# Projection rows streamed through TensorE from the last token to the first, odd weight buffers 128 bytes later

## What is computed

```python
h = rmsnorm(x, norm_mix_g[l])
proj = jnp.einsum('btd,dn->btn', h, w_in[l])
(a_u, a_v, b_q, b_k, b_v, b_z, b_beta, b_alpha, c_q, c_k, c_v, gates) = jnp.split(proj, splits, axis=-1)
...
gates = jax.nn.sigmoid(gates.reshape(B, T, N_BRANCH, D))
```

## Time and profile before

| | us |
|---|---|
| median of 3 runs | 1966.67 |
| lowest, highest | 1965.94, 1969.8 |
| the profiled execution | 1968.53 |
| its span, first to last instruction | 1966.8 |
| TensorE busy in it | 1911.2 |
| VectorE busy | 1093.6 |
| ScalarE busy | 957.7 |
| GpSimd busy | 322.9 |

### The profile page before, as it was taken

The page is one execution under the profiler, slowest core; times in us unless marked ns, Lnnn a source line. Parts: engine busy times, 40 slices in busy tenths (PEclk is TensorE's granted clock), DMA queues, the critical chain, the costliest instruction groups (busy, mean ns, idle before and its releaser), DMA issues.

```text
span 1966.8 us, 26385 instructions
## 1 busy us (share of the span) xinstructions
PE 1911.2 (97%) x9734; PEld 1609.0 (82%) x9734; DVE 1093.6 (56%) x1343; ACT 957.7 (49%) x1301; POOL 322.9 (16%) x483
## 2 busy tenths in 40 slices
PE   6999999999999999999999999999999999999994
PEld 6998888888888888888898788877888888888872
DVE  5113755343442323131246575349988988889865
ACT  5233334222334555554256022135877787877862
POOL 1000000002132232311001000002222222332220
PEclk9999999999999999999999999989999999999997
DMA  6323335799445453534576964246999999999956
GB/s 230 114 91 107 113 122 207 282 350 338 129 155 170 156 183 131 179 115 143 185 225 217 355 228 150 86 192 242 389 381 387 394 390 389 393 387 383 380 202 261
DMA packets 169762, 468.61 MB, mean 238 GB/s; under 512 B 27775, under 2 KB 57423, under 8 KB 163788
## 3 DMA queue, kind: packets, MB, share of 16 engines
q1 hardware_dynamic: 131020, 373.60, 51.3%
q0 software_dynamic: 28288, 74.95, 11.3%
q10 hardware_dynamic: 10368, 18.88, 2.8%
HBM read 378.51 MB, written 105.61 MB: 246 GB/s over the span
## 4 chain that ended last, share of the span: by engine, by line
PE 92%; DVE 3%; DMA 2%; ACT 1%; issue 1%; SPq 0%; POOL 0%; DVEq 0%; POOLq 0%; ACTq 0%
PE psum L668 26%; PE psum L670 26%; PE psum L669 26%; PE psum L2385 2%; PE psum L2361 2%; PE psum L2729 1%; PE psum L2371 1%; PE psum L2398 1%; PE psum L2653 1%; DVE e_l L2135 1%; PE psum L2331 1%; PE psum L2751 1%; PE psum L2789 1%; PE psum L2790 1%; DMA y_raw<-y_scratch 1%
## 5 line engine op out<-in xcount | busy, mean ns | idle before, releaser
L2135 DVE TENSOR_TENSOR e_l<-e_raw,e_h 128x2048 fp32r<-128x2048 f32 x190 | 424.6, 2284 | 34.1 <-ACT e_h L1455 33.7
L668 PE MATMUL psum<-hT_h,w_l 128*128 128x512 f32 x1088 | 432.8, 398 | 0.0
L670 PE MATMUL psum<-hT_h,w_h 128*128 128x512 f32 x1088 | 424.4, 390 | 0.0
L669 PE MATMUL psum<-hT_l,w_h 128*128 128x512 f32 x1088 | 423.8, 390 | 0.0
L1455 ACT CAST e_h<-e_raw 128x2048 fp32r<-128x2048 f32 x190 | 355.9, 1927 | 44.1 <-DMA e_raw<-in_w_e 38.6
L670 PEld LDWEIGHTS psum<-hT_h,w_h 128*128 128x128 f32 x1088 | 204.2, 188 | 43.8
L669 PEld LDWEIGHTS psum<-hT_l,w_h 128*128 128x128 f32 x1088 | 204.7, 188 | 39.7
L668 PEld LDWEIGHTS psum<-hT_h,w_l 128*128 128x128 f32 x1088 | 204.5, 188 | 39.3
L668 PE MATMUL psum<-e_h,xT_l 128*128 128x512 f32 x512 | 202.2, 395 | 1.4 <-DVE xT_l L2141 1.4
L669 PE MATMUL psum<-e_l,xT_h 128*128 128x512 f32 x512 | 199.5, 390 | 0.0
L670 PE MATMUL psum<-e_h,xT_h 128*128 128x512 f32 x512 | 199.3, 389 | 0.0
(11 more groups left out here) (402 smaller groups left out, 3242.8 us busy)
## 6 DMA issues: line engine op xcount, KB each, us to landing
e_raw<-in_w_e SPq DMA_DIRECT2D x192, 1024.0 KB, 11.0
wraw<-in_w_in_t SPq DMA_DIRECT2D x37, 1024.0 KB, 5.1
pt_scratch<-stage SPq DMA_DIRECT2D x52, 512.0 KB, 4.0
gate<-pt_scratch SPq DMA_DIRECT2D x24, 512.0 KB, 6.1
e_rows<-rows_scratch SPq DMA_DIRECT2D x8, 1280.0 KB, 9.5
h_scratch<-xn SPq DMA_DIRECT2D x16, 512.0 KB, 3.6
yg<-expert_rows SPq DMA_DIRECT2D x16, 512.0 KB, 9.7
c_all<-attention_scratch POOLq DMA_DIRECT2D x4, 1560.0 KB, 8.3
```

The lines of the kernel that those rows point to most:

```text
L668: nc.tensor.matmul(out_ap, ll, rh, start=first, stop=False)
L669: nc.tensor.matmul(out_ap, lh, rl, start=False, stop=False)
L670: return nc.tensor.matmul(out_ap, lh, rh, start=False, stop=last)
L2135: nv.tensor_tensor(e_l[:, c], e_raw[:, c], e_h[:, c].bitcast(F32), ALU.subtract).then_inc(s_el13 if c < 4 else s_el2, 1)
```

## The change

Every matmul with tokens moving (chunks 4 to 37) reads its 512 tokens from the last to the first. For chunks 4 to 25 the result is also written to the bank from the last column to the first, so that the bank ends up as before. For the gate chunks the bank is written forward, holds the tokens in reverse, and ScalarE reads it from the last column when it makes the sigmoid. And in odd chunks, those before chunk 4 too, the weights lie 32 floats (128 bytes) further into their buffer. Each engine issues the same instructions in the same order as before; their addresses and the sign of a step differ.

```diff
         def chunk_cols(ap2, c):
 
-            n = CWX if c == 0 else CW
-            return ap2[:, 0:KD * n].rearrange("p (k n) -> p k n", k=KD)
+            n, at = CWX if c == 0 else CW, 32 * (c % 2)
+            return ap2[:, at:at + KD * n].rearrange("p (k n) -> p k n", k=KD)
...
                     if c >= CH_Z:
-                        nc.scalar.activation(o, bank, ACT.Silu if c < CH_GATE else ACT.Sigmoid).then_inc(s_ev, 1)
+                        nc.scalar.activation(o, bank if c < CH_GATE else bank[:, ::-1], ACT.Silu if c < CH_GATE else ACT.Sigmoid).then_inc(s_ev, 1)
...
                     for k in range(4 * half, 4 * half + 4):
-                        ins = mm3(ps[n % 2], wh[:, k, a], wl[:, k, a], hT_h[:, k, tok], hT_l[:, k, tok], k == 0, k == KD - 1)
+                        ins = mm3(ps[n % 2][:, ::-1] if c < CH_GATE else ps[n % 2], wh[:, k, a], wl[:, k, a], hT_h[:, k, tok][:, ::-1], hT_l[:, k, tok][:, ::-1], k == 0, k == KD - 1)
```

## The result

| | before | after |
|---|---|---|
| median, us | 1966.67 (3 runs) | 1987.62 (3 runs) |
| lowest, highest | 1965.94, 1969.8 | 1987.31, 1988.17 |
| profiled execution's span | 1966.8 | 1985.6 |

What follows compares the result with a forecast made beforehand. The prediction took PE to bound the kernel, with the turned matmuls' steps all uncovered. Its four terms, (a) to (d), each taken as 0, left the median forecast at 1966.7 us, range 1930 to 1992.

Steps and rivals of the forecast that it cites:

- rival 2: In all 3264 steps, weights' and moving reads in opposite directions clash more often: +4 to +29 us, middle 1979 us; chance 0.14.
- What bounds the kernel: PE, busy 97% of the 1966.8 us span; 3264 matmuls with hT moving, 226.7 ns each, take 740 us, all uncovered.
- (a): hT read from column 511 down to 0 in 3264 matmuls: taken as 0, bounds -43.4 to +663 us.
- (b): Result written to PSUM from column 511 down in 22 chunks before the gates, 2112 matmuls: taken as 0, at most +429 us.
- (c): In the 12 gate chunks ACT turns the reversed bank when evacuating it: price 0; at twice the time 29 us, off the path.
- (d): In 19 odd chunks w_h and w_l lie 128 bytes later: taken as 0, some 20 ns on ACT and DVE, hidden.
- Rival 1: New addresses loosen a clash of weights' and moving reads in the 13.3 ns beyond the columns: -8 to -43 us; chance 0.23.
- Rival 3: Two neighbours merge into one access only when ascending: +429 us at the PSUM end, +663 at the SBUF end; chance 0.17.

## Why the range held and the forecast did not

The measured time lies in the range because the range had been drawn to take in a rival's band, not because the sum found the cost: the sum had 0, and "slower" by rival 2 had a chance of 0.14.

- **What bounds the kernel**: right. PE is busy throughout, and a change of the step reached the total undiminished: 20.5 us in the stretch, 21 us in the median.
- **(a) Reading backward, taken as 0**: this is the step that failed. It measured up to 6.7 ns on 3264 matmuls: 18.7 us in the stretch and 19.5 us in the median, by the run with the direction alone. The value came from DVE's reversed read and ACT's stepped one, which move about one column per ns; the third rival already said that they do not test a stream of 2.4 columns per ns. I then had no row for the term and chose its middle by likeness of kind. The bounds held, -43 to +663 us, but they were so wide that they forbade little.
- **(b) Writing PSUM backward, taken as 0**: right, by the run with the bank alone turned (ratio 1.0001) and by 233.3 ns in a gate chunk.
- **(c) ScalarE reading the bank backward, taken as 0**: right, 598 ns.
- **(d) The offset, taken as 0**: wrong by itself, 7.4 us, and small here (1.8 us of the stretch) because a reversed stream has lost most of what the offset spoils. I looked for its price in the load's own duration, which stayed at 188 ns, and in its cover. It lay in the step of the matmul beside it. The 264-column rows had shown that steps depend on alignment; I used that for a gain alone.
- **Rival 2** had the sign, the place and the size within its bounds (+4 to +29 us; measured +21, its middle was +12), with 0.14 where the forecast had 0.46. Its mechanism, two streams meeting, did not hold in the form tested: with a load of 32 columns instead of 128 the reversed step stayed at 233.3 ns. That the weights' address, width and step all move the forward stream says that the two reads are not independent; how they meet stays open.
- **Rival 1** (the 13.3 ns can be loosened by other addresses): no; 32 offsets forward and 33 more reversed gave none below 226.7 ns with tokens moving. Its premise that all pairs start on one alignment holds modulo 256 bytes only: the two buffers are 8448 bytes apart. That most of it can vanish is shown by 215.9 ns for a moving operand that stays at one address, which is no use to a product.
- **Rival 3** (pairs merge only when ascending): no at both ends; pairs taken backward step at 226.7. A stream that takes every second float does double the step (453.0 ns), near the 430 ns that the earlier trace rows gave as this rival's price; that is another pattern than the one of the change.
- **The page rules**: the rule of the Trainium skill, page "PSUM — Partial Sum Buffer", section "Specifications (TRN2)", that non-contiguous patterns slow matmuls, does not reach a descending one: the run with the bank turned shows 226.7 ns. The two independent read ports of the Trainium skill, page "TensorE: Matmul & The Clock Gate", section "Step-by-step: what each phase is for", do not keep the weights' address from mattering: 226.7 against 232.4 ns.

What stays open is why. Shown is that the extra time arises where the moving operand is read from SBUF, when runs of 16 bytes descend or the reading jumps back every 64 bytes; that a forward stream loses most of the same time when the weights are moved by most distances below 256 bytes; and that neither the width of the load, nor the direction of the write, nor the length in proportion sets it. The load's own direction was not varied. Nor is it known why the offset lengthens the reversed steps in the odd chunks from 19 to 33 and hardly before. Which resource is shared, and in what turn, no run here tells.

## What to carry to other kernels

A matmul's step from start to start, times its count, is what a change of addresses is worth where TensorE is the bound: a change that moves no instruction made this kernel 1% slower. For fp32r streams of 512 columns like these: read the moving operand upward and keep it aligned with the stationary one as here (by the kernel's layout the starts are 0 or 256 bytes apart modulo 512); if an order must be turned, turn it in blocks of 128 floats, or inside 16 bytes, or on the PSUM side, where it was free. And a row from an engine that moves one column per ns was no evidence for what a stream of 2.4 columns per ns pays.

## What the runs showed of the hardware that I had not expected

- The step of a 512-column fp32r matmul is 226.7 ns in the aligned forward case; at the other 31 offsets of the weights the medians are 229 to 236 ns, except for one chunk each at 16 and 252 bytes that stayed at 227; reversed, 233.3 at nearly all.
- With the moving address standing still it is 215.9 ns, 2.6 beyond the columns.
- A moving step of two floats takes 453.0 ns, twice the plain step.
- Blocks of sixteen floats, each read backward, with a jump ahead between them, take 267.5 ns, more than the whole stream backward.
- Order within 16 bytes, descending PSUM writes (ratio 1.0001) and descending PSUM reads by ScalarE (598 and 588 ns as before) cost nothing that shows.
- A narrower weight load does not shorten the step (233.3 ns reversed at 32 columns), and lengthens it forward, from 227 to between 231 and 233.
